# The latent's variance inside the first query tile, its root and most reciprocals ahead of the first scores, and the softplus chain behind them

## The chip, the cores and the metric

The kernel runs on one core of one Trainium2 chip. The time is the device time of one execution in microseconds (us), and the kernel's time is the median over its runs.

## What is computed

One decoder layer over 1024 tokens with a model width of 2048, in float32. A normalised input goes through one combined projection. Half of the mixing width is a gated linear recurrence; the other half is sparse attention: an indexer scores every causal key for each query, the best 256 are kept, and attention over a compressed key/value latent of width 256 runs over them. The parts that the change touches, cut from the reference:

```python
    h = _rmsnorm(x, norm_g[l])
    proj = jnp.einsum('bsd,de->bse', h, w_in[l])
    xa, ga, q, ckv, gb, qi, ki, wi = jnp.split(proj, IN_SPLITS, axis=-1)
    ...
    c = _rmsnorm(ckv, ckv_norm_g)          # the latent: 1024 x 256
    ki = _layernorm(ki, ik_g, ik_b)        # the indexer's keys: 1024 x 64
    s_idx = jnp.einsum('bqhd,bsd->bqhs', qi_b, ki)
    score = jnp.einsum('bqhs,bqh->bqs', jax.nn.relu(s_idx), wi_b)
    ...
    log_a = -LRU_C * r * jax.nn.softplus(-lam)   # the recurrence's decay, needed much later
```

## The kernel before

Every engine has its own instruction stream, written out by hand, and semaphores tie them together; no scheduler reorders anything.

**Tiles.** The projection is computed transposed, in tiles of 128 output columns for all tokens. Each matmul is done as three in a reduced form of float32 (high half of the weights by high and low half of the activations, and low by high: `triple`, L1039 to L1041). For each weight tile of 2048 rows there are four pieces of four k-steps each. A piece is loaded by SyncE (`w_raw`), cut to its high half by ScalarE (`w_hi`, L743 in `high`), and GpSimd subtracts that from the original (`w_lo`, L663). The cut of a piece for tile t waits until TensorE has used the same piece of tile t−1, since `w_hi` holds one tile. Tile 0 is the indexer's keys and head weights, tiles 1 and 2 the latent (`c_sb`), tiles 3 to 10 the indexer's queries, two heads per tile, for the tokens from 256 up only (two matmul groups of 384 tokens per k-step; the queries before that keep all their keys). Recurrence and attention tiles follow.

**Scores.** A finished query tile stands in PSUM (`PJ`). ScalarE copies its upper and lower 64 rows into the high halves of `stack_a` and `stack_b` (L804, L805), VectorE subtracts to make the low halves (L1442, L1443). Then, while TensorE projects the next tile, it computes the twelve score units of the tile before, one behind each of k-steps 3 to 14 (`score`, L1142 and L1144, called by `step_b`). ScalarE takes the relu of each unit (L814), and VectorE adds it to `scores` with the head's weight (L1467). Score results stand in `X[0]` and `X[1]` by turns, and so do the two relu buffers, so unit m waits for the relu of unit m−2, and the relu of unit m for the sum of unit m−2. The first unit of all waits also for the keys' low half (`ki_done`), for the head weights (`w_nat_s`), and for the latent's root (`c_sd`), because the variance uses `X[1]`.

**Keys.** The layer norm of the keys runs through all engines: mean and variance by TensorE (L1102, L1108), root on ScalarE (L780), reciprocal and product on VectorE (L1413, L1414), scale and high half on ScalarE (L782, L786, L787), low half on VectorE (L1419, L1420).

**Latent.** ScalarE squares both halves, TensorE sums the squares over all 256 columns with four float32 products by a matrix of ones (L1120), behind tile 3 and ahead of tile 4. ScalarE takes the root (L794). `norm_latent(j)` on VectorE does the rest for a quarter of the tokens: a reciprocal (L1451) and two products (L1453). Its four calls stand ahead of score sums 1, 3, 5 and 7 of the first query tile. SyncE stores the latent when all are done, and the second pair of stacks, which lies over it, waits for that store.

**Softplus.** The decay of the recurrence needs softplus of a vector of 8 values per partition: an exponential on ScalarE (L791), for which a table must be loaded, and 14 short dependent steps and one more on VectorE (L1425 to L1435). Its result is first needed when the recurrence begins, at about 340 us. It stands ahead of the latent's root on ScalarE and ahead of the first stacks on VectorE.

Of the kernel before, what the change touches and what calls it, by code (L numbers as in the profile page):

```python
# [30 lines left out]
P = 128  # L31
# [10 lines left out]
CT = C // P  # L42
IH = 16
ID = 64
# [4 lines left out]
NT = 512  # L49
# [3 lines left out]
PIECES = 4  # L53
PK = KT // PIECES


T_KW, T_C, T_QI, T_LRU, T_ATT = 0, 1, 3, 11, 27
# [14 lines left out]
IX_TOKENS = [(0, SKIP, IXN), (NT, SKIP + IXN, IXN)]  # L72
# [18 lines left out]
def off(q):  # L91

    return OFF[q] - OFF[FIRST_SCORED]
# [27 lines left out]
def layer(nc, a, out):  # L121
# [11 lines left out]
    with ctx:  # L133
# [17 lines left out]
        decay = sb("decay", [P, 2, G])  # L151
        sp_t = sb("sp_t", [P, 5, G])
        eps = sb("eps", [P, 1])
# [30 lines left out]
        ki_hi = sB("ki_hi", [P, S], F32R)  # L184
        ki_lo = sB("ki_lo", [P, S], F32R)
# [15 lines left out]
        stack_a, stack_b = [stack_a0, stack_a1], [stack_b0, stack_b1]  # L201
# [81 lines left out]
        PJ, X = PS[0:2], PS[2:4]  # L283
# [20 lines left out]
        bias_st = sem("bias_st")  # L304
# [18 lines left out]
        pj_free = [sem("pj_free0"), sem("pj_free1")]  # L323
# [19 lines left out]
        sp_exp = sem("sp_exp")  # L343
        sp_in = sem("sp_in")
        dec_s = sem("dec_s")
# [57 lines left out]
        def scored(stack, rows):  # L403

            return stack[rows, SKIP:S].rearrange("p (n s) -> p n s", s=IXN)

        def projected(par, rows):

            return PJ[par][rows, :].rearrange("p (n s) -> p n s", s=NT)[:, :, 0:IXN]
# [297 lines left out]
        def _(act):  # L707
# [30 lines left out]
            def high(t, js=range(PIECES)):  # L738

                for j in js:  # L740
                    act.wait_ge(w_in_s[j], 16 * t + 16)
                    act.wait_ge(w_used, 4 * t + j + 1)
                    nc.scalar.activation(w_hi[:, j, :, :], w_raw[:, j, :, :], ACT.Copy).then_inc(w_hi_s, 1)  # L743
# [9 lines left out]
            for i in range(QB):  # L753
# [4 lines left out]
                if FIRST_HALF <= i:  # L758
# [19 lines left out]
            nc.scalar.activation(c_sq[:, 1, :], c_sb[:, 1, :], ACT.Square).then_inc(c_sq_s, 1)  # L778
            act.wait_ge(k_var, 1)
            nc.scalar.activation(k_t[:, :], X[1][0:ID, :], ACT.Sqrt, bias=eps[0:ID, :]).then_inc(k_sd, 1)  # L780
            act.wait_ge(k_nrm, 1)
            nc.scalar.activation(k_t[:, :], kw_sb[0:ID, :], ACT.Identity, scale=k_gb[:, 0:1],  # L782
                                 bias=k_gb[:, 1:2]).then_inc(k_ln, 1)
# [1 line left out]

            nc.scalar.activation(ki_hi[0:ID, :], k_t[:, :], ACT.Copy).then_inc(k_ln, 1)  # L786
            nc.scalar.activation(ki_hi[ID:P, :], k_t[:, :], ACT.Copy).then_inc(k_ln, 1)  # L787
            high(4)

            act.wait_ge(sp_in, 1)  # L790
            nc.scalar.activation(sp_t[:, 1, :], sp_t[:, 0, :], ACT.Exp).then_inc(sp_exp, 1)  # L791
            act.wait_ge(c_var, 1)
            act.wait_ge(bias_st, 16)
            nc.scalar.activation(c_rs[:, :], X[1][:, :], ACT.Sqrt, bias=eps[:, :]).then_inc(c_sd, 1)  # L794
            act.wait_ge(ki_done, 2)
            act.wait_ge(w_tp, 1)

# [18 lines left out]
            def act_b(t, par):  # L816

                stacks(t - 1, 1 - par)
                for j in range(PIECES):
                    high(t + 1, [j])  # L820
                    relus(t - 1, range(min(4 * j, UNITS), min(4 * j + 4, UNITS)))

            act_b(T_QI + 1, 0)
            act.wait_ge(c_st, 16 * CT)
            with act.Fori(0, 3) as i:
                act_b(i * 2 + (T_QI + 2), 1)
# [195 lines left out]
        def _(pe):  # L1022
# [43 lines left out]
            def project_tile(t, par, turn, between=None, parts=ALL_TOKENS, js=range(PIECES), last_part=True):  # L1066
                pe.wait_ge(pj_free[par], turn + 1)
                for j in js:
                    pe.wait_ge(w_lo_s, 4 * t + j + 1 + PIECES)
                    for k in range(PK):  # L1070
                        kt = j * PK + k
                        for at, tok, n in parts:
                            last = triple(PJ[par][:, at:at + n], j, k, slice(tok, tok + n))
                        if k == PK - 1 and last_part:
                            last.then_inc(w_used, 1)
                        if between:
                            between(kt)
# [3 lines left out]
            for i in range(QB):  # L1081
# [5 lines left out]
                else:  # L1087
# [7 lines left out]
                             start=True, stop=True).then_inc(bias_mm, 1)  # L1095
# [16 lines left out]
                last = nc.tensor.transpose(X[0][:, q * IH:(q + 1) * IH], kw_sb[ID:KW, q * P:(q + 1) * P],  # L1112
                                           ident[ID:KW, ID:KW])
            last.then_inc(w_tp, 1)
            project_tile(T_QI, 1, 1, parts=IX_TOKENS)
            pe.wait_ge(c_sq_s, 2)
            pe.wait_ge(k_sd, 1)
            for n in range(2):
                for t in range(CT):
                    last = nc.tensor.matmul(X[1][:, n * NT:(n + 1) * NT], ones_c[:, :],  # L1120
                                            c_sq[:, t, n * NT:(n + 1) * NT], start=(t == 0), stop=(t == CT - 1))
            last.then_inc(c_var, 1)

# [223 lines left out]
        def _(dve):  # L1347
# [9 lines left out]
            def chain(ins):  # L1357

                dve.wait_ge(dve_step, step.did(ins))
# [40 lines left out]
            for q in range(FIRST_SCORED, QB):  # L1400
# [14 lines left out]
            dve.wait_ge(w_tp, 1)  # L1415
            nc.vector.tensor_scalar(w_nat[:, :, :], X[0][:, 0:QB * IH].rearrange("p (q h) -> p q h", h=IH),
                                    IH ** -0.5 * ID ** -0.5, None, ALU.mult).then_inc(w_nat_s, 1)
            dve.wait_ge(k_ln, 3)
            tt(ki_lo[0:ID, :], k_t[:, :], ki_hi[0:ID, :].bitcast(F32), ALU.subtract).then_inc(ki_done, 1)  # L1419
            tt(ki_lo[ID:P, :], k_t[:, :], ki_hi[0:ID, :].bitcast(F32), ALU.subtract).then_inc(ki_done, 1)  # L1420


            dve.wait_ge(sp_exp, 1)
            z, s_, q_, p_ = (sp_t[:, k, :] for k in (1, 3, 4, 0))
            chain(nc.vector.tensor_scalar(s_, z, 2.0, None, ALU.add))  # L1425
            chain(nc.vector.reciprocal(s_, s_))
            chain(tt(s_, s_, z, ALU.mult))
            chain(tt(q_, s_, s_, ALU.mult))
            chain(nc.vector.tensor_scalar(p_, q_, 1.0 / 13, None, ALU.mult))
            for n in (11, 9, 7, 5, 3):  # L1430
                chain(stt(p_, p_, 1.0 / n, q_, ALU.add, ALU.mult))
            chain(stt(p_, p_, 1.0, s_, ALU.add, ALU.mult))
            chain(stt(p_, p_, 2.0, sp_t[:, 2, :], ALU.mult, ALU.add))
            chain(nc.vector.tensor_scalar(decay[:, 0, :], p_, 8.0, None, ALU.mult))
            nc.vector.tensor_scalar(decay[:, 1, :], p_, -8.0, None, ALU.mult).then_inc(dec_s, 1)  # L1435


            def stacks(t, par):

                dve.wait_ge(st_hi, t * 2 - 2 * (T_QI - 1))  # L1440
                a, b = slice(0, ID), slice(ID, P)
                tt(scored(stack_a[par], b), projected(par, a), scored(stack_a[par], a).bitcast(F32), ALU.subtract)  # L1442
                tt(scored(stack_b[par], a), projected(par, b), scored(stack_b[par], b).bitcast(F32), ALU.subtract  # L1443
                   ).then_inc(pj_free[par], 1)

            def norm_latent(j):

                tok = slice(j * S // 4, (j + 1) * S // 4)
                if j == 0:
                    dve.wait_ge(c_sd, 1)  # L1450
                chain(nc.vector.reciprocal(c_rs[:, tok], c_rs[:, tok]))  # L1451
                for t in range(CT):
                    stt(c_sb[:, t, tok], c_sb[:, t, tok], c_g[:, t:t + 1], c_rs[:, tok], ALU.mult, ALU.mult  # L1453
                        ).then_inc(c_done, 1)

            def add_scores(t, first=False):
                for m in range(UNITS):
                    if first and m % 2 == 1 and m < 8:
                        norm_latent(m // 2)
                    q = FIRST_SCORED + m % (UNITS // 2)  # L1460
                    w = (q + 1) * P
                    k = t * UNITS + (m - UNITS * T_QI)
                    dve.wait_ge(ix_relu, k + 3)
                    dve.wait_ge(ix_acc, k + 3)
                    acc = scores[:, off(q):off(q) + w]
                    head = t * 2 + (m // (UNITS // 2) - 2 * T_QI)
                    stt(acc, relu[m % 2][:, 0:w], w_nat[:, q, ds(head, 1)], acc, ALU.mult, ALU.add  # L1467
                        ).then_inc(ix_acc, 1)

            def dve_b(t, par, first=False):  # L1470
                stacks(t - 1, 1 - par)
                add_scores(t - 1, first)

            dve_b(T_QI + 1, 0, first=True)
            with dve.Fori(0, 3) as i:
                dve_b(i * 2 + (T_QI + 2), 1)
                dve_b(i * 2 + (T_QI + 3), 0)
# [226 lines left out]
```

## Time and profile before

| | us |
|---|---|
| median of 3 runs | 1631.76 (1631.68 to 1632.04) |
| the profiled execution | 1631.82 |
| its span | 1630.1 |
| TensorE busy | 1588.7 |
| VectorE busy | 854.2 |
| ScalarE busy | 580.1 |
| GpSimd busy | 431.7 |

The span runs from the first to the last instruction of the profiled execution; the execution's own time is 1.7 us longer. The granted clock of TensorE over the span is 0.995 of full speed. "Idle before" is time in which an engine did nothing, with what ended it. Matmuls overlap, so the time from one start to the next, not the listed duration, is what a matmul costs.

### The profile page before, as it was taken

The page shows a single profiled execution, that of the slowest core. Times are in us where ns is not written, and L with a number is a line of the kernel's source. Part 1 is how long each engine was busy: PE and PEld are TensorE (multiplying, and loading weights), DVE is VectorE, ACT ScalarE, POOL GpSimd, SP SyncE. Part 2 cuts the span into 40 slices and gives each one's busy share as a digit, 9 for nine tenths or more (in the row PEclk, how much of TensorE's full clock was granted, in tenths as well). Part 3 has the DMA queues.
Part 4 walks back from the last instruction along what each step waited for, and adds up shares of the span by engine and source line. Part 5 has one row for each costly group of instructions (what it writes and reads, how often), then busy time and mean ns, then how long its engine had stood idle before and what let it go on. Part 6 is the DMA issues. An engine that isn't in the chain of part 4 may idle for free.

```text
span 1630.1 us, 21564 instructions
## 1 busy us (share of the span) xinstructions
PE 1588.7 (97%) x7595; PEld 1324.9 (81%) x7595; DVE 854.2 (52%) x1498; ACT 580.1 (36%) x845; POOL 431.7 (26%) x289
## 2 busy tenths in 40 slices
PE   7999999999999999999999999999998899999998
PEld 7788999888888888888888888777776788888886
DVE  6427555577777877875555555376777100031003
ACT  6325555433444443332111111355555222232321
POOL 2222222222222222222222222110010344444650
PEclk9999999999999999999999999999999999999999
DMA  7212111122212122223222221321222522237322
GB/s 262 83 49 72 46 45 39 33 55 62 61 55 65 33 63 68 68 84 97 77 71 77 71 77 51 110 85 61 71 73 81 217 94 100 94 101 298 132 85 103
DMA packets 132312, 141.38 MB, mean 87 GB/s; under 512 B 8519, under 2 KB 103849, under 8 KB 129961
## 3 DMA queue, kind: packets, MB, share of 16 engines
q1 hardware_dynamic: 130728, 136.55, 26.2%
q0 software_dynamic: 1536, 4.20, 0.8%
q8 instruction: 30, 0.49, 0.1%
q14 instruction: 18, 0.14, 0.0%
HBM read 116.08 MB, written 24.64 MB: 86 GB/s over the span
## 4 chain that ended last, share of the span: by engine, by line
PE 83%; issue 8%; DVE 4%; ACT 2%; POOL 1%; DMA 1%; DVEq 0%; SPq 0%; ACTq 0%; POOLq 0%
PE ps L1039 17%; PE ps L1040 17%; PE ps L1041 17%; PE ps L1315 6%; PE ps L1317 6%; PE ps L1316 6%; PE ps L1142 2%; PE ps L1144 2%; PE ps L1256 2%; PE ps L1220 2%; PE ps L1233 1%; PE ps L1342 1%; PE ps L1341 1%; PE ps L1340 1%; PE ps L1240 1%
## 5 line engine op out<-in xcount | busy, mean ns | idle before, releaser
L1039 PE MATMUL ps<-hT_hi,w_lo 128*128 128x512 f32 (+1 forms) x1344 | 511.9, 381 | 3.2 <-POOL w_lo L663 3.2
L1040 PE MATMUL ps<-hT_lo,w_hi 128*128 128x512 f32 (+1 forms) x1344 | 509.9, 379 | 0.0
L1041 PE MATMUL ps<-hT_hi,w_hi 128*128 128x512 f32 (+1 forms) x1344 | 509.8, 379 | 0.0
L663 POOL TENSOR_TENSOR w_lo<-w_raw,w_hi 128x512 fp32r<-128x512 f32 x168 | 240.7, 1436 | 758.4 <-ACT w_hi L743 758.4
L1039 PEld LDWEIGHTS ps<-hT_hi,w_lo 128*128 128x128 f32 x1344 | 252.6, 188 | 48.6 <-issue 5.4
L1040 PEld LDWEIGHTS ps<-hT_lo,w_hi 128*128 128x128 f32 x1344 | 252.7, 188 | 43.4 <-issue 0.2
L1041 PEld LDWEIGHTS ps<-hT_hi,w_hi 128*128 128x128 f32 x1344 | 252.7, 188 | 42.7
L743 ACT ACTIVATE w_hi<-w_raw 128x512 fp32r<-128x512 f32 x168 | 104.8, 629 | 479.0 <-PE ps L1041 472.7
L1315 PE MATMUL ps<-wo_hi,hT_lo 128*128 128x512 f32 x448 | 175.2, 391 | 3.1 <-DVE hT_lo L1584 3.1
L1643 DVE TENSOR_TENSOR res<-ps,res 128x512 f32<-128x512 f32 x32 | 21.8, 691 | 295.7 <-PE ps L1317 245.0
L1316 PE MATMUL ps<-wo_lo,hT_hi 128*128 128x512 f32 x448 | 174.8, 390 | 0.0
L1317 PE MATMUL ps<-wo_hi,hT_hi 128*128 128x512 f32 x448 | 174.7, 390 | 0.0
L1492 DVE MATCH_REPLACE8 scores<-top,scores 128x384 f32<-128x384 f32 (+2 forms) x192 | 165.8, 876 | 0.0
L1487 DVE MAX8 top<-scores 128x8 f32<-128x384 f32 (+2 forms) x192 | 155.3, 878 | 1.3 <-DVE sg L1524 0.6
L698 POOL TENSOR_TENSOR wo_lo<-wo_raw,wo_hi 128x1024 fp32r<-128x1024 f32 x48 | 116.1, 2420 | 148.3 <-ACT wo_hi L972 148.3
L1467 DVE SCALAR_TENSOR_TENSOR scores<-relu,w_nat,scores 128x384 f32<-128x384 f32 (+2 forms) x96 | 94.7, 996 | 79.2 <-ACT relu L814 79.0
L972 ACT ACTIVATE wo_hi<-wo_raw 128x1024 fp32r<-128x1024 f32 x48 | 50.8, 1060 | 191.6 <-PE ps L1317 191.6
L814 ACT ACTIVATE relu<-ps 128x384 f32<-128x384 f32 (+2 forms) x96 | 72.9, 760 | 80.1 <-PE ps L1144 65.1
L1315 PEld LDWEIGHTS ps<-wo_hi,hT_lo 128*128 128x128 f32 x448 | 84.5, 189 | 20.6 <-issue 3.3
L1317 PEld LDWEIGHTS ps<-wo_hi,hT_hi 128*128 128x128 f32 x448 | 84.5, 189 | 17.8
L1316 PEld LDWEIGHTS ps<-wo_lo,hT_hi 128*128 128x128 f32 x448 | 84.5, 189 | 17.5
L1531 DVE TENSOR_TENSOR rg<-ps,ig 128x1024 f32<-128x1024 f32 x8 | 9.8, 1224 | 157.9 <-ACT ig L892 139.9
(190 smaller groups left out, 1825.8 us busy)
## 6 DMA issues: line engine op xcount, KB each, us to landing
w_raw<-in_w_in SPq DMA_DIRECT2D x168, 256.0 KB, 2.8
wo_raw<-in_w_out SPq DMA_DIRECT2D x64, 512.0 KB, 3.6
xin<-in_x SPq DMA_DIRECT2D x8, 1024.0 KB, 6.0
res<-in_x SPq DMA_DIRECT2D x8, 1024.0 KB, 10.6
out<-res SPq DMA_DIRECT2D x16, 512.0 KB, 5.0
y_lru_dram<-sg SPq DMA_DIRECT2D x8, 512.0 KB, 2.8
q_dram<-av SPq DMA_DIRECT2D x8, 512.0 KB, 3.8
gate_dram<-rg SPq DMA_DIRECT2D x8, 512.0 KB, 4.3
```

The costliest lines, as they stand in the source:

```text
L663: nc.gpsimd.tensor_tensor(w_lo[:, j, :, :], w_raw[:, j, :, :], w_hi[:, j, :, :].bitcast(F32), ALU.subtract).then_inc(w_lo_s, 1)
L698: nc.gpsimd.tensor_tensor(wo_lo[:, j % 2, :, :], wo_raw[:, j % 4, :, :], wo_hi[:, j % 2, :, :].bitcast(F32), ALU.subtract).then_inc(wo_lo_ ...
L743: nc.scalar.activation(w_hi[:, j, :, :], w_raw[:, j, :, :], ACT.Copy).then_inc(w_hi_s, 1)
L1039: nc.tensor.matmul(o, wlo, hi, start=(kt == 0), stop=False)
L1040: nc.tensor.matmul(o, whi, lo, start=False, stop=False)
L1041: return nc.tensor.matmul(o, whi, hi, start=False, stop=(kt == KT - 1))
L1315: nc.tensor.matmul(o, hT_lo[:, kt, tok], wo_hi[:, j % 2, k, :], start=(kt == 0), stop=False)
L1316: nc.tensor.matmul(o, hT_hi[:, kt, tok], wo_lo[:, j % 2, k, :], start=False, stop=False)
L1317: last = nc.tensor.matmul(o, hT_hi[:, kt, tok], wo_hi[:, j % 2, k, :], start=False, stop=(kt == KT - 1))
L1467: stt(acc, relu[m % 2][:, 0:w], w_nat[:, q, ds(head, 1)], acc, ALU.mult, ALU.add).then_inc(ix_acc, 1)
L1487: found = step.did(nc.vector.max(top8[:, q, :], scores[:, off(q):off(q) + (q + 1) * P]))
L1492: marked = step.did(nc.vector.match_replace(left, top8[:, q, :], left, TAKEN))
```

## The change

Three things are moved; none is added or taken away but one table load. On TensorE the four products of the variance are issued behind k-step 5 of tile 3 instead of behind the tile. On ScalarE the first weight piece of tile 4 is cut and the latent's root is taken ahead of the scaling of the keys; the exponential of the softplus goes behind the whole first pass of scores. On VectorE one pass of `norm_latent` goes ahead of the keys' low halves and two behind them, the fourth ahead of score sum 1, and the softplus steps go behind the first pass of score sums, ahead of the next stacks.

```diff
@@ ScalarE
             nc.scalar.activation(k_t[:, :], X[1][0:ID, :], ACT.Sqrt, bias=eps[0:ID, :]).then_inc(k_sd, 1)
+            high(4, [0])
+            act.wait_ge(c_var, 1)
+            act.wait_ge(bias_st, 16)
+            nc.scalar.activation(c_rs[:, :], X[1][:, :], ACT.Sqrt, bias=eps[:, :]).then_inc(c_sd, 1)
             act.wait_ge(k_nrm, 1)
...
             nc.scalar.activation(ki_hi[ID:P, :], k_t[:, :], ACT.Copy).then_inc(k_ln, 1)
-            high(4)
-
-            act.wait_ge(sp_in, 1)
-            nc.scalar.activation(sp_t[:, 1, :], sp_t[:, 0, :], ACT.Exp).then_inc(sp_exp, 1)
-            act.wait_ge(c_var, 1)
-            act.wait_ge(bias_st, 16)
-            nc.scalar.activation(c_rs[:, :], X[1][:, :], ACT.Sqrt, bias=eps[:, :]).then_inc(c_sd, 1)
+            high(4, range(1, PIECES))
...
             act_b(T_QI + 1, 0)
+            act.wait_ge(sp_in, 1)
+            nc.scalar.activation(sp_t[:, 1, :], sp_t[:, 0, :], ACT.Exp).then_inc(sp_exp, 1)
             act.wait_ge(c_st, 16 * CT)
@@ TensorE
-            project_tile(T_QI, 1, 1, parts=IX_TOKENS)
...
+            def latent_variance(kt):
+
+                if kt != PK + 1:
+                    return
+                pe.wait_ge(c_sq_s, 2)
+                pe.wait_ge(k_sd, 1)
+                for n in range(2):
+                    for t in range(CT):
+                        last = nc.tensor.matmul(X[1][:, n * NT:(n + 1) * NT], ones_c[:, :],
+                                                c_sq[:, t, n * NT:(n + 1) * NT], start=(t == 0), stop=(t == CT - 1))
+                last.then_inc(c_var, 1)
+
+            project_tile(T_QI, 1, 1, between=latent_variance, parts=IX_TOKENS)
@@ VectorE
+            norm_latent(0)
             dve.wait_ge(k_ln, 3)
             tt(ki_lo[0:ID, :], k_t[:, :], ki_hi[0:ID, :].bitcast(F32), ALU.subtract).then_inc(ki_done, 1)
             tt(ki_lo[ID:P, :], k_t[:, :], ki_hi[0:ID, :].bitcast(F32), ALU.subtract).then_inc(ki_done, 1)
-
-
+            norm_latent(1)
+            norm_latent(2)
...
+                for m in range(UNITS):
+                    if first and m == 1:
+                        norm_latent(3)
...
+            dve_b(T_QI + 1, 0, first=True)
             dve.wait_ge(sp_exp, 1)
             z, s_, q_, p_ = (sp_t[:, k, :] for k in (1, 3, 4, 0))
             chain(nc.vector.tensor_scalar(s_, z, 2.0, None, ALU.add))
...
             nc.vector.tensor_scalar(decay[:, 1, :], p_, -8.0, None, ALU.mult).then_inc(dec_s, 1)
...
-                for m in range(UNITS):
-                    if first and m % 2 == 1 and m < 8:
-                        norm_latent(m // 2)
...
-            dve_b(T_QI + 1, 0, first=True)
             with dve.Fori(0, 3) as i:
```

The order of instructions on ScalarE from the keys' high halves to the first stacks, before (`w_hi` is a weight cut, `sp_t` the exponential, `c_rs` the latent's root):

```order
L787 ACTIVATE ki_hi<-k_t 64x1024
L743 ACTIVATE w_hi<-w_raw 128x512 x4
L791 ACT_TABLE_LOAD
L791 ACTIVATE sp_t<-sp_t 128x8
L794 ACT_TABLE_LOAD
L794 ACTIVATE c_rs<-ps,eps 128x1024
L804 ACTIVATE stack_a<-ps 64x768
L805 ACTIVATE stack_b<-ps 64x768
```

and the same engine now, from the root of the keys to the first stacks:

```order
L780 ACTIVATE k_t<-ps,eps 64x1024
L743 ACTIVATE w_hi<-w_raw 128x512
L784 ACTIVATE c_rs<-ps,eps 128x1024
L786 ACTIVATE k_t<-kw_sb,par_t 64x1024
L790 ACTIVATE ki_hi<-k_t 64x1024
L791 ACTIVATE ki_hi<-k_t 64x1024
L743 ACTIVATE w_hi<-w_raw 128x512 x3
L802 ACTIVATE stack_a<-ps 64x768
L803 ACTIVATE stack_b<-ps 64x768
```

The root of the latent has moved ahead of the keys' scaling (L786), and neither a table load nor the exponential stands ahead of the first stacks. They stand now where ScalarE goes from the first pass of scores into the loop over the next tiles:

```order
L812 ACTIVATE relu<-ps 128x1024
L743 ACTIVATE w_hi<-w_raw 128x512
L823 ACT_TABLE_LOAD
L823 ACTIVATE sp_t<-sp_t 128x8
L825 UNCONDITIONAL_BRANCH
L825 ISA
L800 ISA
L802 ACTIVATE stack_a<-ps 64x768
L803 ACTIVATE stack_b<-ps 64x768
```

Load and exponential have come between the last weight cut of the pass and the stacks that the loop begins with. On VectorE, at the same place, from the last score sum of the first pass to the stacks of the loop:

```order
L1459 SCALAR_TENSOR_TENSOR scores<-relu,w_nat,scores 128x1024
L1469 TENSOR_SCALAR sp_t<-sp_t 128x8
L1470 RECIPROCAL sp_t<-sp_t 128x8
L1471 TENSOR_TENSOR sp_t<-sp_t 128x8
L1472 TENSOR_TENSOR sp_t<-sp_t 128x8
L1473 TENSOR_SCALAR sp_t<-sp_t 128x8
L1475 SCALAR_TENSOR_TENSOR sp_t<-sp_t 128x8 x5
...
L1479 TENSOR_SCALAR decay<-sp_t 128x8
L1481 UNCONDITIONAL_BRANCH
L1481 ISA
L1444 TENSOR_TENSOR stack_a<-ps,stack_a 64x768
```

Before, the last score sum was followed by the loop's branch and its stacks; the fifteen short steps stood ahead of the first stacks.

## Rows read from the trace of the kernel before

**Rows 1.** The page, busy time of TensorE (us, share of the span, instructions).

```profile
PE 1588.7 (97%) x7595; PEld 1324.9 (81%) x7595; DVE 854.2 (52%) x1498; ACT 580.1 (36%) x845; POOL 431.7 (26%) x289
```

**Rows 2.** Timeline, TensorE, tile 3 to first score: start, us, operation [idle before <-releaser].

```profile
112.19 0.34 PE L1040 MATMUL ps<-hT_lo,w_hi 128*128 128x384 f32 x1
...
128.65 3.60 PE L1120 MATMUL ps<-c_sq,ones_c 128*128 128x512 f32 x8
...
136.07 0.34 PE L1041 MATMUL ps<-hT_hi,w_hi 128*128 128x384 f32 x1
137.02 0.44 PE L1142 MATMUL ps<-ki_lo,stack_a 128*128 128x384 f32 x1 [0.61 <-DVE stack_b L1443]
```

**Rows 3.** Timeline, TensorE, a wait inside tile 4 and tile 5's first matmul.

```profile
153.02 0.50 PE L1142 MATMUL ps<-ki_lo,stack_b 128*128 128x512 f32 x1 [0.80 <-ACT relu L814]
...
159.22 0.33 PE L1039 MATMUL ps<-hT_hi,w_lo 128*128 128x384 f32 x1
```

**Rows 4.** Timeline, TensorE, first score beside tile 5; tile 6's first matmul and score.

```profile
163.97 0.44 PE L1142 MATMUL ps<-ki_lo,stack_a 128*128 128x384 f32 x1 [0.42 <-DVE stack_b L1443]
...
184.57 0.33 PE L1039 MATMUL ps<-hT_hi,w_lo 128*128 128x384 f32 x1
...
189.03 0.44 PE L1142 MATMUL ps<-ki_lo,stack_a 128*128 128x384 f32 x1
```

**Rows 5.** Timeline, ScalarE, key scaling, softplus, and the stacks of two later tiles.

```profile
121.11 1.24 ACT L782 ACTIVATE k_t<-kw_sb,par_t 64x1024 f32<-64x1024 f32 x1 [7.86 <-DVE kw_sb L1414]
...
129.56 1.28 ACT L791 ACT_TABLE_LOAD   x1
130.85 0.21 ACT L791 ACTIVATE sp_t<-sp_t 128x8 f32<-128x8 f32 x1
...
159.48 0.63 ACT L743 ACTIVATE w_hi<-w_raw 128x512 fp32r<-128x512 f32 x1
160.23 0.81 ACT L804 ACTIVATE stack_a<-ps 64x768 fp32r<-64x768 f32 x1
...
184.77 0.63 ACT L743 ACTIVATE w_hi<-w_raw 128x512 fp32r<-128x512 f32 x1
185.31 0.79 ACT L804 ACTIVATE stack_a<-ps 64x768 fp32r<-64x768 f32 x1
```

**Rows 6.** Timeline, VectorE, key low half, softplus steps, first stacks, one norm pass.

```profile
125.81 2.20 DVE L1420 TENSOR_TENSOR ki_lo<-k_t,ki_hi 64x1024 fp32r<-64x1024 f32 x1
131.09 0.54 DVE L1425 TENSOR_SCALAR sp_t<-sp_t 128x8 f32<-128x8 f32 x1 [3.08 <-ACT sp_t L791]
131.67 0.20 DVE L1426 RECIPROCAL sp_t<-sp_t 128x8 f32<-128x8 f32 x1
...
134.12 0.17 DVE L1435 TENSOR_SCALAR decay<-sp_t 128x8 f32<-128x8 f32 x1
135.05 0.95 DVE L1442 TENSOR_TENSOR stack_a<-ps,stack_a 64x768 fp32r<-64x768 f32 x1 [0.75 <-ACT stack_b L805]
...
138.84 1.74 DVE L1451 RECIPROCAL c_rs<-c_rs 128x256 f32<-128x256 f32 x1
...
141.41 0.75 DVE L1467 SCALAR_TENSOR_TENSOR scores<-relu,w_nat,scores 128x512 f32<-128x512 f32 x1
```

**Rows 7.** Timeline, GpSimd, the last weight piece cut at a tile's end.

```profile
185.48 1.94 POOL L663 TENSOR_TENSOR w_lo<-w_raw,w_hi 128x512 fp32r<-128x512 f32 x1 [6.05 <-ACT w_hi L743]
```

**Rows 8.** Timeline, TensorE, two long waits; then stretches: length, PE busy, clock, DMA, GB/s.

```profile
45.68 0.47 PE L1039 MATMUL ps<-hT_hi,w_lo 128*128 128x512 f32 x1 [2.81 <-POOL w_lo L663]
1272.13 0.79 PE L1315 MATMUL ps<-wo_hi,hT_lo 128*128 128x512 f32 x1 [3.07 <-DVE hT_lo L1584]
...
46.72:50.10 3.38, 3.38 (x9) 0.51 0.32 80
15.95:22.73 6.78, 4.98 (x28) 0.50 0.29 102
1272.13:1275.47 3.34, 3.34 (x8) 0.51 0.75 260
```

More of the change, by code:

```diff
@@ L1114, in _ @@
             last.then_inc(w_tp, 1)
-            project_tile(T_QI, 1, 1, parts=IX_TOKENS)
[L1116 to L1122, printed above, removed]
+            def latent_variance(kt):
[9 more added lines that the diff above has]
+            project_tile(T_QI, 1, 1, between=latent_variance, parts=IX_TOKENS)
             def score(t, par, turn, ms, first=False):
@@ L1417, in _, with norm_latent @@
                                     IH ** -0.5 * ID ** -0.5, None, ALU.mult).then_inc(w_nat_s, 1)
+            def norm_latent(j):
+                tok = slice(j * S // 4, (j + 1) * S // 4)
+                if j == 0:
+                    dve.wait_ge(c_sd, 1)
+                chain(nc.vector.reciprocal(c_rs[:, tok], c_rs[:, tok]))
+                for t in range(CT):
+                    stt(c_sb[:, t, tok], c_sb[:, t, tok], c_g[:, t:t + 1], c_rs[:, tok], ALU.mult, ALU.mult
+                        ).then_inc(c_done, 1)
+            norm_latent(0)
             dve.wait_ge(k_ln, 3)
@@ L1420, in _, with stacks, add_scores, dve_b @@
             tt(ki_lo[ID:P, :], k_t[:, :], ki_hi[0:ID, :].bitcast(F32), ALU.subtract).then_inc(ki_done, 1)
+            norm_latent(1)
+            norm_latent(2)
+            def stacks(t, par):
+                dve.wait_ge(st_hi, t * 2 - 2 * (T_QI - 1))
+                a, b = slice(0, ID), slice(ID, P)
+                tt(scored(stack_a[par], b), projected(par, a), scored(stack_a[par], a).bitcast(F32), ALU.subtract)
+                tt(scored(stack_b[par], a), projected(par, b), scored(stack_b[par], b).bitcast(F32), ALU.subtract
+                   ).then_inc(pj_free[par], 1)
+            def add_scores(t, first=False):
+                for m in range(UNITS):
+                    if first and m == 1:
+                        norm_latent(3)
+                    q = FIRST_SCORED + m % (UNITS // 2)
+                    w = (q + 1) * P
+                    k = t * UNITS + (m - UNITS * T_QI)
+                    dve.wait_ge(ix_relu, k + 3)
+                    dve.wait_ge(ix_acc, k + 3)
+                    acc = scores[:, off(q):off(q) + w]
+                    head = t * 2 + (m // (UNITS // 2) - 2 * T_QI)
+                    stt(acc, relu[m % 2][:, 0:w], w_nat[:, q, ds(head, 1)], acc, ALU.mult, ALU.add
+                        ).then_inc(ix_acc, 1)
+            def dve_b(t, par, first=False):
+                stacks(t - 1, 1 - par)
+                add_scores(t - 1, first)
+            dve_b(T_QI + 1, 0, first=True)
             dve.wait_ge(sp_exp, 1)
@@ L1435, in _ @@
             nc.vector.tensor_scalar(decay[:, 1, :], p_, -8.0, None, ALU.mult).then_inc(dec_s, 1)
[L1438 to L1456, printed above, removed]
-                for m in range(UNITS):
-                    if first and m % 2 == 1 and m < 8:
-                        norm_latent(m // 2)
[L1460 to L1472, printed above, removed]
-            dve_b(T_QI + 1, 0, first=True)
             with dve.Fori(0, 3) as i:
```

## The prediction

> **What bounds the kernel now.** The page's busy times come first: TensorE is busy for 97% of the span [rows 1], so a change of order on ScalarE and VectorE counts only where TensorE waits for it. The timeline of TensorE around the first query tiles comes next, since everything that the diff moves lies between 111 and 164 us. The reader should see four things in it.
>
> The tile of query weights that comes first (tile 3, at tokens from 256 up) issues a matmul every 0.173 us: 95 steps lead from 112.19 to 128.65, where the variance begins [rows 2]. The variance takes the engine until the next tile's work flows again, about 3.44 us. Of tile 4 the first four k-steps (24 matmuls, 4.16 us) need nothing from the scores. The 24th of these starts at 136.07, so the first score could start at 136.24; it starts at 137.02, when VectorE has written the low half of the stacks [rows 2]. Later in the same tile TensorE waits for a relu, 0.80 us idle ahead of 153.02 [rows 3], and once more by less; those relus are late because four passes of the latent's norm stand between the score sums on VectorE, each pass some 2.57 us from 138.84 to 141.41 [rows 6]. Tile 4 ends and tile 5 begins at 159.22 [rows 3], and the first score of tile 5's stretch comes at 163.97, 4.75 us behind that end. One tile on, the tile ends at about 184.57 and the score comes at 189.03 [rows 4], 4.46 us behind it.
>
> The last number is the one to keep. From the end of a tile the stacks of its projections are made by ScalarE (two copies) and VectorE (two subtractions), one after the other, and TensorE has only 4.16 us of other work. This chain is already longer than its cover. Whatever is put into it delays the first score of that stretch one for one.
>
> **The change part by part.**
> Removed stalls. From the first score to the end of its tile it is 137.02 to 159.22, 22.20 us; the same stretch one tile later, with no norm in it, is 163.97 to 184.57, 20.60 us [rows 2 to 4]. In the changed kernel one pass of the norm is left, ahead of the second score sum. Before, a pass stood there too, and no relu was late until the third and fourth had come. So the gain is 22.20 − 20.60 = **−1.60 us**.
>
> The variance inside tile 3. Its four products are issued either way, and nothing stands between it and its place: by the count it starts 35 steps behind 112.19, at 118.26, and ends near 121.9. TensorE's sum up to the first score is the same, so **0**. The weight piece that ScalarE cuts ahead of the root waits for tile 3's first four k-steps, near 116.1, when ScalarE was idle; it costs nothing while that idle time, up to 121.11 [rows 5], is there.
>
> The root ahead of the key's norm. The key's scaling started at 121.11 [rows 5]; it now stands behind the root, which ends near 122.95, so it and all behind it come 1.84 us later. The last low half of the keys ended at 125.81 + 2.20 = 128.01 [rows 6] and now ends near 129.85. Behind it stand two norm passes of 2.57 us, which end near 135.0. The stacks on VectorE started at 135.05 [rows 6]. ScalarE's two copies no longer wait for a table and a root, and end near 134.7: the last cut at 132.3, 0.75 us from cut to copy, and two copies of 0.8 [rows 5]. So VectorE becomes what is late, at almost the time at which the old stacks started: **+0.05 us**, with −0.4 (only ScalarE's chain counts) and +0.6 (passes held up by GpSimd's cuts) as ends. I take the middle because the old and new VectorE sums agree within 0.1.
>
> The softplus chain behind the first score sums. This is the large term. On ScalarE the exponential now stands behind the last weight piece of tile 5, which is cut only when tile 4 has ended, and ahead of the next stacks. In times from the end of a tile (184.57): the cut starts at +0.20 [rows 4, 5]; the table load begins 0.65 later (the 0.63 of the cut and a gap), the exponential 1.29 later (129.56 to 130.85), and VectorE's first step 0.24 after that (130.85 to 131.09) [rows 5, 6]. That is +2.38. GpSimd's subtraction for that last piece runs to 187.42 [rows 7], +2.85, and the first step of the chain took 0.54 us where the last took 0.17 [rows 6]; I take it that it ends with GpSimd's work, at +2.89. The other steps, 131.67 to 134.12 + 0.17, are 2.62 us, with a gap of 0.04 ahead: +5.55. Then come the stacks, 1.97 us from their start to the first score (135.05 to 137.02) [rows 2, 6]: **the score comes at +7.52 where it came at +4.75, a loss of 2.8 us**. ScalarE's copies are done by then (load and exponential push them by about 1.5 us, to +4.0), so VectorE's short steps are what is late. Ends of this term: +2.3 if the first step isn't held up and the exit of ScalarE is as quick as at 185.31, +3.2 if the entry of the loop, now directly behind the short chain, adds some 0.3 that the old trace hides in idle time.
>
> Before, both parts cost nothing visible: load and exponential ran at 129.56 to 131.06, in ScalarE's wait for the variance, and the short steps in VectorE's wait for the stacks. That cover is gone. The second table load of before, back to the root's table, disappears, but it stood beside the variance.
>
> Here a rule speaks against the change. In rows 5 a load lasts 1.28 us and the exponential follows it directly: 129.56 to 130.85. The Trainium skill, "ScalarE: Activation LUTs", section "What ACT_TABLE_LOAD costs", adds about 1.38 us of drain to each switch of set; by that the loss would be larger by about a microsecond. The trace shows no such time beside this load, so the sum goes without it.
>
> TensorE's clock. The new stall lasts from +4.16 to +7.52, about 3.4 us of idle time in one piece. Where the trace of before has such pieces, the clock falls: behind 2.81 us of idle time it went to half, 1.2 GHz, at 46.72 to 50.10, and behind 3.07 us it was at half for 1272.13 to 1275.47 [rows 8]. Some 3.3 us at half rate do the work of 1.65. The longest such piece, 15.95 to 22.73 with 4.98 us of work in it [rows 8], costs 2.5. Both stalls are shorter than the new one, so I take a fall, and of it **+1.6 us**, with 0 and 2.5 as ends.
>
> DMA issues keep their order on the queue of SyncE; the latent's store is free some 11 us earlier, and the loads queued behind it too, which gates nothing. Everything behind this stretch follows TensorE and moves with it.
>
> Sum: −1.60 + 0.05 + 2.8 + 1.6 = **+2.85 us**. The profiled execution took 1631.82 us for a span of 1630.1, and the median of the three runs is 1631.76, which is the same for this purpose. 1631.82 + 2.85 gives **1634.7 us**.
>
> **The rivals.**
> (1) The clock does not fall. Two stalls are few, and nothing in the rows says that the length of a wait alone decides it. Against it: 2.81 us were enough. Then 1631.8 + 1.25 = 1633.1.
> (2) Slower. The table switch drains ScalarE ahead of the exponential when the engine comes straight out of a weight cut. With about 1.4 us more in the chain, less the 0.4 or so that would then no longer be spent waiting for GpSimd, the first score comes 1.0 later: 1635.7. It decides from about 0.3 us on, since the forecast lies 0.3 below the bound of slower. Against it is the load of rows 5, which did follow a weight cut. This is the page's rule of above taken as a mechanism.
> (3) The norm's passes hold up the first stacks. If GpSimd's cuts hold the low half of the keys and both passes, VectorE reaches the stacks a microsecond late and the first score with them: 1635.7. For it: the 2.20 us of one low half [rows 6].
> (4) The change hides all that it moves: the short chain finds idle time, and only the stalls go, 1631.8 − 1.55 = 1630.3. For this the exponential would have to run before tile 4 ends; the order says it doesn't.
>
> **How the numbers follow.** A measurement of this kernel can tell about 0.2%, 3.3 us, from no change; so slower begins at 1635.0 and faster below 1628.5. Forecast 0.57, (1) 0.25, (2) 0.10, (3) 0.05, (4) 0.03. Of the forecast's own range, 1634.0 to 1635.6, a fifth lies above 1635.0; with (2) and nearly all of (3) that makes 0.25 for slower. Case (4) is not over the bound, and I leave 0.03 for faster. The range takes in (1) with its lower ends, 1632.0, and the longer fall of the clock or (2), 1636.3. The later fall at 1272 us could come out otherwise once the program is shifted, which would give 1.7 back; the low end holds that together with the forecast.
>
> **What would show it.** In the changed kernel's trace: the variance at 118 us; the first score still near 137.0; no idle time for relus until tile 4 ends near 157.6; then a table load at about 158.4, the short steps up to about 163, the first score of tile 5's stretch near 165.1, with some 3.4 us idle ahead of it and a granted clock of 0.5 within a few us; later tiles as before. If that idle time is below 2 us, the softplus term is wrong; if the first score comes after 137.6, the norm term is.

## The result and the profile after

| | before | changed |
|---|---|---|
| median, 11 runs each, us | 1631.9 | 1636.01 |
| lowest and highest | 1630.36 to 1633.34 | 1633.86 to 1637.58 |
| the profiled execution | 1631.82 | 1635.85 |
| its span | 1630.1 | 1634.2 |

The ratio is 1.0024, with a 95% interval of 1.0017 to 1.0032. The change made the kernel slower, by 4.1 us. The forecast was 1634.7 with a range of 1632.0 to 1636.3, so the direction and the mechanism were right in the main, and the time was 1.3 us above its likeliest value.

The timeline of TensorE in the changed kernel (start, us, operation, idle time before it with what ended it) shows where the time went. Its lines answer to [rows 2 to 4].

```profile
112.53 0.34 PE L1040 MATMUL ps<-hT_lo,w_hi 128*128 128x384 f32 x1
...
118.60 3.60 PE L1123 MATMUL ps<-c_sq,ones_c 128*128 128x512 f32 x8
...
137.43 0.44 PE L1147 MATMUL ps<-ki_lo,stack_a 128*128 128x384 f32 x1 [0.67 <-DVE stack_b L1445]
...
158.04 0.33 PE L1039 MATMUL ps<-hT_hi,w_lo 128*128 128x384 f32 x1
...
166.49 0.49 PE L1147 MATMUL ps<-ki_lo,stack_a 128*128 128x384 f32 x1 [4.13 <-DVE stack_b L1445]
...
193.09 0.44 PE L1147 MATMUL ps<-ki_lo,stack_a 128*128 128x384 f32 x1
```

Read it from mark to mark, beside the kernel before:

| stretch | before | changed | difference |
|---|---|---|---|
| start of tile 3 to first score | 24.83 | 24.90 | +0.07 |
| first score to end of tile 4 | 22.20 | 20.61 | −1.59 |
| end of tile 4 to the next first score | 4.75 | 8.45 | +3.70 |
| that score to the one a tile later | 25.06 | 26.60 | +1.54 |

The sum is +3.72. Another 0.34 lies ahead of tile 3 (112.53 for 112.19), in the start with its loads; the two spans differ by 4.1. The program is the same there, and this mark lies anywhere from 110.93 to 112.55 in the other runs, so the 0.34 is scatter and no work of the change. The later steps take 25.05 to 25.08 us in both, up to the last one of the loop.

The waits for relus are gone. In their place one wait has grown to 4.13 us. What fills it is seen on ScalarE:

```profile
158.30 0.63 ACT L743 ACTIVATE w_hi<-w_raw 128x512 fp32r<-128x512 f32 x1
158.95 1.28 ACT L823 ACT_TABLE_LOAD   x1
160.24 0.21 ACT L823 ACTIVATE sp_t<-sp_t 128x8 f32<-128x8 f32 x1
160.36 0.79 ACT L802 ACTIVATE stack_a<-ps 64x768 fp32r<-64x768 f32 x1
161.18 0.81 ACT L803 ACTIVATE stack_b<-ps 64x768 fp32r<-64x768 f32 x1
```

on VectorE:

```profile
160.49 0.23 DVE L1469 TENSOR_SCALAR sp_t<-sp_t 128x8 f32<-128x8 f32 x1 [0.94 <-ACT sp_t L823]
160.75 0.20 DVE L1470 RECIPROCAL sp_t<-sp_t 128x8 f32<-128x8 f32 x1
...
163.01 0.17 DVE L1478 TENSOR_SCALAR decay<-sp_t 128x8 f32<-128x8 f32 x1
163.21 1.19 DVE L1479 TENSOR_SCALAR decay<-sp_t 128x8 f32<-128x8 f32 x1
164.43 0.95 DVE L1444 TENSOR_TENSOR stack_a<-ps,stack_a 64x768 fp32r<-64x768 f32 x1
```

and on GpSimd:

```profile
159.01 1.68 POOL L663 TENSOR_TENSOR w_lo<-w_raw,w_hi 128x512 fp32r<-128x512 f32 x1 [6.05 <-ACT w_hi L743]
163.11 1.26 POOL L663 TENSOR_TENSOR w_lo<-w_raw,w_hi 128x512 fp32r<-128x512 f32 x1 [2.42 <-ACT w_hi L743]
```

ScalarE's copies are ready at 161.99, and VectorE reaches the stacks at 164.43. VectorE's last short step took 1.19 us where its twin ahead of it took 0.17. GpSimd's subtraction had begun at 163.11, just before it, and ended at 164.37, just before it ended. Behind the wait the clock fell. Stretches of the changed kernel (length, busy time of PE, PEld, DVE, ACT and POOL with counts, granted clock, DMA share, GB/s):

```profile
162.20:166.40 4.20, 0.17 (x1) 0.00 (x0) 3.93 (x8) 0.63 (x1) 1.26 (x1) 1.00 0.34 90
166.90:170.10 3.20, 3.20 (x11) 3.00 (x10) 0.62 (x1) 0.49 (x1) 0.00 (x0) 0.50 0.00 0
```

A granted clock of 0.50 is 1.2 GHz, half of what the stretch ahead of it has.

### The profile page after: what moved, and what is told of

Read it like the earlier page. It is cut to its first block, busy times and chain, and to the rows that moved or that the text cites. A ratio compares the mean times of both kernels' runs of the same rounds, so it can differ in the third digit from the quotient of the medians.

```text
span 1634.2 us, 21563 instructions
## 1 busy us (share of the span) xinstructions
PE 1590.3 (97%) x7595; PEld 1327.0 (81%) x7595; DVE 855.1 (52%) x1498; ACT 579.0 (35%) x844; POOL 431.5 (26%) x289
## 4 chain that ended last, share of the span: by engine, by line
PE 84%; issue 8%; DVE 4%; ACT 2%; POOL 1%; DMA 1%; DVEq 0%; SPq 0%; ACTq 0%; POOLq 0%
PE ps L1039 17%; PE ps L1040 17%; PE ps L1041 17%; PE ps L1320 6%; PE ps L1322 6%; PE ps L1321 6%; PE ps L1147 2%; PE ps L1149 2%; PE ps L1261 2%; PE ps L1225 2%; PE ps L1238 1%; PE ps L1347 1%; PE ps L1346 1%; PE ps L1345 1%; PE ps L1245 1%
```

## The experiments

Theory A was the prediction's: the loss is the softplus between the end of tile 4 and the next stacks, plus the clock, and the gain is the norm passes out of the score sums. Its rival B laid the loss on the variance inside the tile and the passes ahead of the first stacks. Each experiment below is the changed kernel with one edit, unless it says otherwise. Ratios are to the kernel before, whose runs beside them had medians of 1631.7 to 1631.9 us.

| experiment | median us | ratio, 95% interval |
|---|---|---|
| own_slot | 1630.66 | 0.9994 (0.9985 to 1.0003) |
| softplus_only | 1637.85 | 1.0043 (1.0029 to 1.0057) |
| cut_waits | 1634.85 | 1.0018 (1.0009 to 1.0027) |
| filled | 1633.87 | 1.0016 (1.0007 to 1.0025) |
| exp_only_there | 1631.33 | 0.9999 (0.999 to 1.0008) |
| passes_back | 1631.16 | 0.9995 (0.9986 to 1.0004) |
| spread | 1630.76 | 0.9994 (0.9985 to 1.0003) |
| stacks_first | 1627.89 | 0.9978 (0.9968 to 0.9987) |
| best | 1627.2 | 0.9969 (0.9957 to 0.9981) |
| before_swap | 1629.85 | 0.9989 (0.998 to 0.9998) |

### The softplus in another place: own_slot

```diff
 def act_b(t, par, first=False):
     stacks(t - 1, 1 - par)
+    if first:
+        act.wait_ge(sp_in, 1)
+        nc.scalar.activation(sp_t[:, 1, :], sp_t[:, 0, :], ACT.Exp).then_inc(sp_exp, 1)
...
 def add_scores(t, first=False):
     for m in range(UNITS):
         if first and m == 1:
             norm_latent(3)
+        if first and m == 7:
+            softplus()
...
```

> The changed kernel, with the softplus taken out of the critical place: the exponential behind the first stacks on ScalarE, where it idled for 2.0 us, and the short steps ahead of score sum 7 of the first pass on VectorE. Theory A (what costs is the softplus between the end of tile 4 and the next stacks): the first score beside tile 5 comes 4.5 to 4.8 us behind the tile's end again instead of 8.45, no stall over 1 us is left from 137 to 190 us, the clock does not fall, and the time is the kernel before minus the removed stalls, about 1630.4, 5.6 below the changed kernel. Theory B (the variance inside the tile and the norm passes ahead of the first stacks are what costs): at least 2 us of the slowdown stay, 1634 or more.

`softplus()` holds the short steps of VectorE as they were. It came out at 1630.66. The first score beside tile 5 stands 4.52 us behind the tile's end, and the whole step takes 25.15 us:

```profile
137.03 0.44 PE L1148 MATMUL ps<-ki_lo,stack_a 128*128 128x384 f32 x1 [0.68 <-DVE stack_b L1462]
...
162.18 0.44 PE L1148 MATMUL ps<-ki_lo,stack_a 128*128 128x384 f32 x1 [0.20 <-DVE stack_b L1462]
```

Variance, root and norm passes are all where the change has them, and the slowdown is gone. B falls. Table load and exponential run from 134.47 to 135.97, in ScalarE's idle time behind the first stacks, and 0.48 us of it are left. Against the kernel before the gain is about 1 us by the medians, which the interval does not separate from none. The trace shows it: from tile 3's mark to the first score beside tile 5 are 50.05 us for 51.78 before, 1.73 less. Some 0.9 of this is lost again late in the profiled execution, where a stretch at half rate stands at 1251 us that the kernel before doesn't have there (see the last section).

### Only the softplus moved: softplus_only

The kernel before, with the exponential behind `act_b(T_QI + 1, 0)` and the short steps behind `dve_b(T_QI + 1, 0, first=True)`.

> The kernel before, with nothing changed but the place of the softplus: exponential and short steps behind the first pass of scores, as in the changed kernel. Theory A: the whole loss and none of the gain: the first score beside tile 5 comes 3.7 us later, the clock falls for another 1.6, about 1637.2. Theory B: 1632 to 1633.

1637.85 us: the loss without the gain. The first score beside tile 5 comes 8.45 us behind the tile's end, as in the changed kernel, and the two waits for relus are there as before (0.79 and 0.26 us):

```profile
152.28 0.50 PE L1142 MATMUL ps<-ki_lo,stack_b 128*128 128x512 f32 x1 [0.79 <-ACT relu L812]
156.41 0.50 PE L1142 MATMUL ps<-ki_lo,stack_b 128*128 128x512 f32 x1 [0.26 <-ACT relu L812]
166.94 0.68 PE L1142 MATMUL ps<-ki_lo,stack_a 128*128 128x384 f32 x1 [4.13 <-DVE stack_b L1430]
```

The step behind it takes 27.19 us, 2.13 more than an undisturbed one: the clock's fall cost 0.6 more here than in the changed kernel, about what the time lies above the expected one. The fall was longer: from 164.95 to 171.70 the granted clock is 0.50, with 4.76 us of TensorE's work in it, where the changed kernel has some 3.4 us.

### What made the last step long: cut_waits

```diff
 def act_b(t, par, wait=False):
     stacks(t - 1, 1 - par)
+    if wait:
+        act.wait_ge(dec_s, 1)
     for j in range(PIECES):
         high(t + 1, [j])
```

> The changed kernel, with one wait more: ScalarE cuts the first weight piece behind the stacks of a tile only when the softplus steps are done, so that GpSimd's subtraction does not run beside the last of these steps. If GpSimd's access to the memory is what made that last step 1.19 us long, it takes 0.17 now, the first score beside tile 5 comes about 1.0 us earlier, and the time is about 1635.0, with a stall of 3.1 us that still lets the clock fall. If the 1.19 us belong to the branch into the loop that stands behind the step, it stays at 1.1 to 1.2 us and the time at 1636.0.

1634.85 us. VectorE and GpSimd in that stretch:

```profile
161.98 0.17 DVE L1481 TENSOR_SCALAR decay<-sp_t 128x8 f32<-128x8 f32 x1
162.22 0.95 DVE L1446 TENSOR_TENSOR stack_a<-ps,stack_a 64x768 fp32r<-64x768 f32 x1
```

```profile
163.08 1.26 POOL L663 TENSOR_TENSOR w_lo<-w_raw,w_hi 128x512 fp32r<-128x512 f32 x1 [3.60 <-ACT w_hi L743]
```

The step takes 0.17 us and the stacks follow 0.07 us behind its end, the entry into the loop included, so that entry costs next to nothing. The first score comes 7.45 us behind the tile's end, 1.00 earlier. What held the step was GpSimd's subtraction. The Trainium skill names such a contention ("GPSIMD Engine Reference", section "8. Key points"): GpSimd shares its interfaces to SBUF with VectorE and contends with instructions of two inputs there or in a mode that uses both ports. The trace agrees that the two engines contend; which mode the step was in no run here shows. The stacks, which read PSUM, weren't held: the second subtraction of VectorE took 0.96 us from 163.18, beside GpSimd's, as it did in the changed kernel without one beside it.

### The clock by itself: filled

```diff
     if m == 0 and fill:
+        pe.wait_ge(ix_relu, k + 1)
+        for _ in range(fill):
+            nc.tensor.matmul(X[0][:, 0:NT], hT_hi[:, 0, 0:P], hT_hi[:, 0, 0:NT], start=True, stop=True)
```

with `fill=16` for the tile beside tile 5 alone, which is taken out of TensorE's loop for that.

> The changed kernel, with 16 matmuls of 512 columns issued by TensorE in the long wait ahead of the first score beside tile 5, into the score bank that the first score then overwrites; their result is used by nothing. They take 3.6 us of the 4.3 us wait. Theory A with the clock: the granted clock stays at 1.00 through 160 to 175 us and the time falls by the 1.6 us that half rate cost, to about 1634.4. If the clock's fall costs nothing by itself, 1636.0 as in the changed kernel.

1633.87 us, 2.1 below the changed kernel and 0.5 below the expected time. TensorE in the same place, and a stretch of the windows:

```profile
161.13 3.83 PE L1140 MATMUL ps<-hT_hi 128*128 128x512 f32 x16
165.36 0.45 PE L1151 MATMUL ps<-ki_lo,stack_a 128*128 128x384 f32 x1 [0.40 <-DVE stack_b L1451]
```

```profile
163.00:166.00 3.00, 2.60 (x13) 1.93 (x11) 2.26 (x3) 0.00 (x0) 0.33 (x1) 1.00 0.32 87
166.00:169.00 3.00, 3.00 (x18) 2.82 (x18) 1.26 (x2) 1.09 (x2) 0.00 (x0) 1.00 0.00 0
```

The score still comes 8.39 us behind the end of the tile, but the clock stays at 1.00 and the step behind it takes 24.98 us instead of 26.60. So 1.6 us of the slowdown were the clock, which did not fall once TensorE had work in the wait.

### ScalarE's part alone: exp_only_there

The exponential stays where the change has it; `softplus()` is called ahead of score sum 5 of the last pass.

> The changed kernel, with the table load and the exponential left where the change has them, between the last weight cut and the stacks, and only VectorE's short steps moved away, into the last pass of score sums. It prices ScalarE's part alone. By the rows (0.65 to the load, 1.29, 0.12) the copies start 1.6 us later than without it and the first score beside tile 5 comes 5.9 to 6.0 us behind the tile's end, 1.4 later than the 4.46 of an undisturbed tile; the wait of 1.8 us is too short to let the clock fall; about 1632.1. If a table switch costs another 1.4 us of drain, the score comes 7.3 us behind the end and the time is 1633.5 or, with the clock down, 1635.

1631.33 us, 0.8 below the expected time. ScalarE at the place, and TensorE behind it:

```profile
156.70 0.63 ACT L743 ACTIVATE w_hi<-w_raw 128x512 fp32r<-128x512 f32 x1
157.35 1.28 ACT L823 ACT_TABLE_LOAD   x1
158.65 0.21 ACT L823 ACTIVATE sp_t<-sp_t 128x8 f32<-128x8 f32 x1
158.76 0.79 ACT L802 ACTIVATE stack_a<-ps 64x768 fp32r<-64x768 f32 x1
```

```profile
162.49 0.44 PE L1147 MATMUL ps<-ki_lo,stack_a 128*128 128x384 f32 x1 [1.72 <-DVE stack_b L1461]
```

The score comes 6.05 us behind the tile's end, 1.59 later than in an undisturbed tile. From the load's start at 157.35 to the copy's at 158.76 are 1.41 us, and 0.02 lie between the weight cut's end and the load. No drain of another 1.4 us, which rival (2) had, fits in. The Trainium skill ("ScalarE: Activation LUTs", section "What ACT_TABLE_LOAD costs") adds such a drain of about 1.38 us to each switch; this trace does not agree. A wait of 1.72 us left the clock alone (the next step takes 25.07). By difference to the changed kernel the short steps on VectorE cost 2.40 us of the score's delay, of which 1.00 was GpSimd.

### What the gain was: passes_back

The four calls of `norm_latent` again ahead of score sums 1, 3, 5 and 7; the exponential behind the first stacks, the short steps in the last pass.

> The changed kernel, with the four passes of the norm put back ahead of score sums 1, 3, 5 and 7, the softplus steps in the last pass, and the exponential behind the first stacks; the variance stays inside tile 3 and the root ahead of the key's scaling. If the gain of the change is the passes out of the score sums, the two waits for relus come back (1.6 us from the first score to the end of its tile), and only the earlier stacks stay as a gain, up to 0.5: 1631.2. If moving the variance is what gains, no relu is waited for and the time is 1630 or less.

1631.16 us, as the first case says. Both waits are back (0.79 and 0.26), and the first step takes 26.95 us, which is exactly the kernel before:

```profile
136.88 0.44 PE L1148 MATMUL ps<-ki_lo,stack_a 128*128 128x384 f32 x1
...
152.88 0.50 PE L1148 MATMUL ps<-ki_lo,stack_b 128*128 128x512 f32 x1 [0.79 <-ACT relu L812]
...
163.83 0.44 PE L1148 MATMUL ps<-ki_lo,stack_a 128*128 128x384 f32 x1 [0.40 <-DVE stack_b L1459]
```

The first score stands 4.43 us behind the end of tile 3 where it stood 4.99 in the changed kernel: without norm passes ahead of them the first stacks wait for ScalarE alone. The variance and the root moved forward gain a little of their own. From tile 3's mark to the first score are 24.33 us here, and 24.75 in softplus_only, where the exponential is gone from this place as well but the variance still stands behind the tile; the kernel before has 24.83. That is 0.4 to 0.5 us, which the interval of the run times does not separate from none. The larger gain is the early passes, which this move makes possible.

### A version that beats both: spread, stacks_first, best and before_swap

**spread** has one norm pass fewer ahead of the first stacks (passes 2 and 3 ahead of sums 1 and 5) and the short steps ahead of sum 9.

> The version with the softplus in its own slot, with one norm pass fewer ahead of the first stacks: passes 2 and 3 ahead of score sums 1 and 5, the softplus steps ahead of sum 9. VectorE then waits for ScalarE's copies at the first stacks instead of being late itself: first score about 0.45 us earlier, no wait for a relu (four sums recover one pass), 1630.2. If a pass or the short steps ahead of a later sum hold up a relu, a wait of 0.3 to 1 us appears and the gain is gone.

1630.76 us, and both halves of the expectation came true. The first score stood 4.42 behind the tile's end, but the short steps ahead of sum 9 held up the last relu by 1.88 us of idle time, and with it the weight cut and the stacks:

```profile
156.19 1.03 ACT L812 ACTIVATE relu<-ps 128x1024 f32<-128x1024 f32 x1 [1.88 <-DVE scores L1477]
157.12 0.62 ACT L743 ACTIVATE w_hi<-w_raw 128x512 fp32r<-128x512 f32 x1
```

The next first score came 5.15 us behind the end.

**stacks_first** changes the order that [rows 5] had shown in every tile: weight cut, then copies.

```diff
     def act_b(t, par, first=False):
         stacks(t - 1, 1 - par)
...
-        for j in range(PIECES):
+        high(t, [PIECES - 1])
+        for j in range(PIECES - 1):
             high(t + 1, [j])
...
```

It is the spread version otherwise; the last cut of tile 4 leaves its old place, and the pass over the last tile is followed by the one cut that is then missing.

> The spread version, and in every tile the last weight cut behind the stacks' copies instead of ahead of them. The rows say that the chain from a tile's end to the first score is 4.46 us against 4.17 of other work, and that the cut takes 0.54 of it. If that chain bounds the start of the scores in each tile, the 0.3 us of wait per tile disappear in seven tiles and the time falls by 2.0 to 2.5, to about 1627.9. If VectorE or GpSimd (whose subtraction then runs beside VectorE's) takes the place of the cut, no more than 1 us is gained.

1627.89 us, 2.9 below spread. Behind the first step (25.71) they take 24.7 us instead of 25.06.

**best** puts the pieces together: the short steps in the last pass, passes as in spread, copies ahead of the last cut.

> What the runs so far point to, together: variance inside tile 3, norm passes 2 and 3 ahead of score sums 1 and 5, the exponential behind the first stacks, the short softplus steps in the last pass of score sums, and in every tile the stacks' copies ahead of the last weight cut. No step stands between a tile's end and its stacks, and no sum holds up a relu: first score 4.17 us behind the end of each tile from 3 on, every step of the score pass 24.7 us, and about 1627.0 (0.9 below the version whose short steps ahead of sum 9 held up relus). If that 0.88 us wait had another cause, the first step stays near 25.7.

1627.2 us, a ratio of 0.9969 (0.9957 to 0.9981) to the kernel before. TensorE has no listed wait between 100 and 345 us, and every first score up to 283 us stands 4.16 or 4.17 us behind its tile's end. Its first scores:

```profile
160.23 0.34 PE L1150 MATMUL ps<-ki_lo,stack_a 128*128 128x384 f32 x1
...
184.89 0.33 PE L1150 MATMUL ps<-ki_lo,stack_a 128*128 128x384 f32 x1
...
209.57 0.33 PE L1150 MATMUL ps<-ki_lo,stack_a 128*128 128x384 f32 x1
```

**before_swap** is the kernel before with the new order of copies and cut alone.

> The kernel before, with nothing but the stacks' copies put ahead of the last weight cut in every tile. If the gain of that order is independent of the change, the steps behind the first take 24.7 us instead of 25.06 and the time is 1629.0 to 1629.5; the first step keeps its waits for relus. If it needs the rest of the change, nothing or less than 1 us is gained.

1629.85 us (0.9989, 0.998 to 0.9998): the first step keeps its 26.97, the second takes 24.76, and those behind it 24.66 to 24.69 us here too. About 2 us of the 4.7 that best gains belong to this order and need nothing of the change; the rest comes with the earlier root and passes and the softplus elsewhere, and its parts are not priced one by one in this order.

## Why the prediction was right, and where it fell short

**Removed stalls**, −1.60 predicted: −1.59 measured, and passes_back brings them back.

**The variance inside tile 3**, 0 predicted: it started at 118.60, 6.07 us behind the mark that had been 112.19, as counted (118.26 there), and passes_back, 0.5 us ahead of the kernel before at the first score, shows that it costs nothing.

**The root ahead of the key's norm**, +0.05 predicted: +0.07 measured. VectorE was late by itself, as said; passes_back and spread reach the first score 0.57 earlier once it isn't.

**The softplus chain**, 2.8 predicted with ends of 2.3 and 3.2: 3.70 measured. This is the step that fell short, by size and beyond its upper end. Up to the last short step everything stood within 0.1 of the sum or earlier: exponential at +2.20 for +2.14, first step at +2.45 for +2.38, last step begun at +5.17 for about +5.4. The prediction had GpSimd hold up the first step, by the subtraction that ends a tile, to +2.89; it was done at +2.68. It did not look at the next subtraction: ScalarE, once past its copies, cuts the first piece of the next tile while VectorE is still in the chain, and GpSimd follows at 163.11. Before the change no short step stood there. cut_waits prices it at 1.00 us. The term is 0.93 too small in all: 1.02 for the last step, 0.03 for the gap behind it and 0.09 for the stretch from stacks to score (2.06 us where 1.97 was taken from the first stacks), less 0.21 for the first step. The term's upper end held 0.3 for the entry into the loop, which took next to nothing.

**TensorE's clock**, +1.6 predicted: +1.54 in the step behind the stall, and 1.6 back with the wait filled. The size was right. The reason given, that shorter stalls had been followed by a fall, was weaker than it looked: waits of 3.08 us stand in these runs without one (last section). Rival (1), no fall, is out. So are rival (3), since the passes did not hold the first stacks beyond the sum, and rival (4), since the exponential ran only behind the end of tile 4 and the score came 3.70 us later.

**Rival (2)**, the drain of a table switch, would have given a time, 1635.7, closer to the measured one than the forecast's. It is not what happened: in exp_only_there load and exponential cost 1.59 us of delay together. That the total agreed with a rival whose mechanism was absent is a reason to read the stretches and not only the sum. For the same reason some luck is in the range: the time lies in its upper part, which was put there for a longer fall of the clock or for this rival, and neither came; the term that filled it was the one that had been taken too small.

**The sum**: +2.85 predicted, +3.72 by the marks of the trace, +4.1 by medians. The profiled executions differ by 4.03, which is the 3.72 and the 0.34 ahead of tile 3. That the medians differ by as much is in part chance; single executions of one kernel differ by 3 us or more between lowest and highest here.

## What to carry to other kernels

When work is moved off one wait, look at the engines' next hand-over before placing it: the end of a tile, where two engines pass results on in turn and the third has only a fixed amount of other work, was a bad place for a step that nothing needs soon (8.45 us to the first score for 4.46). The middle of a score pass was a good one as long as no relu was held up: ahead of sum 7 (own_slot) and of sum 5 of the last pass (best) the short steps cost nothing, ahead of sum 9 (spread) they did. Ahead of such a hand-over even the order of two instructions on ScalarE, copy or weight cut first, was worth 2 us (before_swap); the change with its softplus put elsewhere gains about 1 us by the medians (own_slot), which is not clear of the noise, and 1.7 us by the trace. A stall on TensorE also has a second price when the clock falls behind it: 1.5 to 2.1 us here on top of the idle time.

## What the runs showed that had not been expected

A step of 8 values per partition on VectorE took 1.19 us, seven times its 0.17, because it began 0.10 us after a subtraction on GpSimd. It happened again in own_slot, in the middle of the pass, where it cost nothing:

```profile
151.41 1.19 DVE L1452 SCALAR_TENSOR_TENSOR sp_t<-sp_t 128x8 f32<-128x8 f32 x1
152.63 0.17 DVE L1453 SCALAR_TENSOR_TENSOR sp_t<-sp_t 128x8 f32<-128x8 f32 x1
```

```profile
151.28 1.29 POOL L663 TENSOR_TENSOR w_lo<-w_raw,w_hi 128x512 fp32r<-128x512 f32 x1 [5.45 <-ACT w_hi L743]
```

The step ends with the subtraction and doesn't share its time. All of the long steps of this chain are of this kind: 0.54 us in the kernel before, 1.20 in softplus_only, 1.21 in filled, 1.14 and 0.94 in before_swap, each ending 0.02 to 0.03 us behind the end of a subtraction on GpSimd. The chain of short steps (fourteen in all in every trace, not fifteen) takes 2.8 to 2.9 us from its first start to its last end where no subtraction holds it (cut_waits, spread, exp_only_there), and 3.9 where one holds a step for its whole length.

And the clock. With the stall beside tile 5 it fell each time that the stall lasted 3.13 us or more (cut_waits, changed kernel, softplus_only), between 2.0 us ahead of the stall's end and 0.3 us behind it, at a price of 1.50 to 2.13 us in the next step. With a stall of 1.72 us it did not. But the length of a wait alone does not decide it. Later in the program every version has nearly the same waits, and they come out both ways. Ahead of an attention matmul stands one of 2.23 us:

```profile
1252.91 1.77 PE L1233 MATMUL ps<-kT,qT 128*128 128x512 f32 x4 [2.23 <-ACT pT L926]
```

In the kernel before the granted clock stays at 1.00 behind it (1252.90 to 1256.20); in own_slot, behind the same 2.23 us, it is 0.50 from 1251.40 to 1254.70. The wait of 3.07 us ahead of the output projection, with half rate behind it in [rows 8], is 3.08 us in filled, and from 1275.50 to 1278.80 the clock there is 1.00. In exp_only_there half rate began 1.3 us (1047.80 to 1051.10 at 0.50) behind the end of a wait of only 1.61 us. What decides beside the length stays open here. Executions of one kernel differ in it too: those of own_slot had a mean granted clock of 0.993 with 1630.62 to 1631.36 us, or 0.995 with 1629.58 to 1630.27. A fall 1000 us behind a change can thus come or not, at up to 1.7 us (3.4 us at half rate). Two kernels that differ by 1 or 2 us are better compared stretch by stretch than by their medians.
